# The attention output of a streaming encoder step kept with channels on partitions: gate rows are scaled and turned instead of values

## The reference, cut to what matters

```
oa = _swept_attention(qa, ka, va, _causal, F)          # branch a: softmax over all earlier keys
ob = _banded_sink_attention(qb, kb, vb, sinks)         # branch b: a window of 128 keys back
oc = _swept_attention(qc, kc, vc, _chunk_causal)       # branch c
br = [oa * silu(ga), ob * silu(gb), oc * silu(gc)]     # (tokens, 512) each
up = einsum('bsnw,nwd->bsnd', br, w_br)                # three (512 x 1024) products
mixed = (sigmoid(gates) * up).sum(axis=2)
y = mixed @ w_o ;  x = LayerNorm(alpha * x + y)
```

## Time and profile before

| | |
|---|---|
| median of 3 runs | 3697.83 us (3694.39 to 3703.88) |
| profiled execution, its own time | 3709.84 us |
| its span | 3708.2 us |
| PE (TensorE matmul) busy | 3331.5 us, 90% |
| DVE (VectorE) / ACT (ScalarE) busy | 1433.3 us, 39% / 882.9 us, 24% |
| prompt attention, matmuls first to last | 643.38 to 1420.59 us and 2469.65 to 3242.87 us |
| up projection, SyncE's first load to the last matmul | 1582.54 to 1758.55 us in the first layer |

### The profile page before, as it was taken

How to read it: one execution, slowest core, us unless ns; L and a number is a source line. 1 busy time by engine, 2 the same in 40 slices (tenths; PEclk the granted TensorE clock), 3 DMA queues, 4 the chain that set the end, 5 groups by cost and what they waited for, 6 DMA issues and landing times. The chain is left out here.

```text
span 3708.2 us, 52576 instructions
## 1 busy us (share of the span) xinstructions
PE 3331.5 (90%) x20738; PEld 2665.9 (72%) x20738; DVE 1433.3 (39%) x3527; ACT 882.9 (24%) x1976; POOL 172.6 (5%) x118
## 2 busy tenths in 40 slices
PE   0999987999999996989969999789999999978988
PEld 0788874787777774668758888657777877745877
DVE  5114233444444442354631143334444444424546
ACT  1221211333222332220212212123332233312010
POOL 0000000100110100000000000010011110000000
PEclk9999998999999997989979999889999999978999
DMA  5322215322333317653442222352223332096533
GB/s 196 105 94 88 84 55 175 97 68 56 85 93 86 84 40 183 206 224 125 151 153 85 94 94 67 102 158 71 64 74 85 90 90 66 30 250 224 196 134 108
DMA packets 405676, 419.75 MB, mean 113 GB/s; under 512 B 155072, under 2 KB 314688, under 8 KB 403072
## 3 DMA queue, kind: packets, MB, share of 16 engines
q1 hardware_dynamic: 371600, 376.88, 32.9%
q10 hardware_dynamic: 33840, 39.66, 3.3%
HBM read 291.17 MB, written 127.64 MB: 113 GB/s over the span
## 5 line engine op out<-in xcount | busy, mean ns | idle before, releaser
L1053 PE MATMUL att_gacc<-att_gwh,keep_xh 128*128 128x256 f32 x1728 | 507.5, 294 | 8.3 <-POOL att_gwl L973 8.3
L351 PE MATMUL proj_acc<-proj_wh,keep_xh 128*128 128x512 f32 (+1 forms) x1296 | 502.3, 388 | 12.4 <-DVE proj_wl L326 12.4
L353 PE MATMUL proj_acc<-proj_wh,keep_xl 128*128 128x512 f32 (+1 forms) x1296 | 500.9, 387 | 0.0
L352 PE MATMUL proj_acc<-proj_wl,keep_xh 128*128 128x512 f32 (+1 forms) x1296 | 500.9, 386 | 0.0
L1055 PE MATMUL att_gacc<-att_gwh,keep_xl 128*128 128x256 f32 x1728 | 488.9, 283 | 0.0
L1054 PE MATMUL att_gacc<-att_gwl,keep_xh 128*128 128x256 f32 x1728 | 488.3, 283 | 0.0
L1079 ACT ACTIVATE att_p<-att_ss,att_stat 128x257 f32<-128x257 f32 (+9 forms) x384 | 249.2, 649 | 684.1 <-DVE att_stat L1129 678.2
L1007 PE MATMUL att_ss<-att_kt,att_qt 64*128 64x256 f32 (+9 forms) x1024 | 377.6, 470 | 1.2 <-DVE att_kt L1064 1.2
L1053 PEld LDWEIGHTS att_gacc<-att_gwh,keep_xh 128*128 128x128 f32 x1728 | 329.1, 190 | 24.3 <-issue 10.6
L1054 PEld LDWEIGHTS att_gacc<-att_gwl,keep_xh 128*128 128x128 f32 x1728 | 328.9, 190 | 0.0
L1055 PEld LDWEIGHTS att_gacc<-att_gwh,keep_xl 128*128 128x128 f32 x1728 | 328.2, 190 | 0.0
(11 more groups left out here) (271 smaller groups left out, 4341.4 us busy)
## 6 DMA issues: line engine op xcount, KB each, us to landing
scratch_gates<-att_gout SPq DMA_DIRECT2D x216, 128.0 KB, 1.7
up_gates<-scratch_gates SPq DMA_DIRECT2D x18, 1536.0 KB, 7.6
proj_raw<-in_w_in SPq DMA_DIRECT2D x48, 512.0 KB, 3.7
att_graw<-in_w_in SPq DMA_DIRECT2D x48, 512.0 KB, 3.7
str_ka<-in_cache_a_kT SPq DMA_DIRECT2D x16, 1024.0 KB, 8.6
str_va<-in_cache_a_v SPq DMA_DIRECT2D x16, 1024.0 KB, 5.3
scratch_sg<-proj_out SPq DMA_DIRECT2D x54, 256.0 KB, 2.0
up_br<-scratch_br SPq DMA_DIRECT2D x54, 256.0 KB, 8.0
```

The costliest lines, as they stand in the source:

```text
L351: nc.tensor.matmul(bank, hi, wh[:, u, kt, 0:w], start=kt == 0, stop=False)
L352: nc.tensor.matmul(bank, hi, wl[:, u, kt, 0:w], start=False, stop=False)
L353: mm = nc.tensor.matmul(bank, lo, wh[:, u, kt, 0:w], start=False, stop=kt == KT - 1)
L1053: nc.tensor.matmul(gacc[:, 0:GW], hi, gwh[:, n % 2, k, :], start=k == 0, stop=False)
```

## The change

In attention, `back` is gone. Instead, at the end of each odd turn VectorE takes both reciprocals at once and multiplies the gate rows of the pair with them (`sgr`, tokens on partitions). A new entry `gate(n, a)` transposes `sgr` on TensorE into `tr` and ScalarE copies it to `sgt`. A new entry `mix(n, a)` is one VectorE product of `oo`, straight from PSUM, with `sgt`, into `o`, which now holds channels by tokens. `gate` stands right behind the turn of the next even sub, ahead of the score; `mix` stands behind the score, where `back` was. The store goes to a new scratch tensor `brt` (1536 channels by 1024 tokens). In the up projection the eight prompt tiles are loaded from `brt` with channels on partitions by one DMA each, and ScalarE and VectorE split them straight from SBUF; only the ninth tile is still transposed.

```
@@ attention_order
         for m in range(SUBS):
+            before = None if m % 2 or m + n == 0 else (n, m // 2 - 1) if m else (n - 1, PT - 1)
             order.append(("turn", n, m))
+            if before:
+                order.append(("gate", *before))
             (score as before)
-            if m % 2 == 0 and m:
-                order.append(("back", n, m // 2 - 1))
-            elif m == 0 and n:
-                order.append(("back", n - 1, PT - 1))
+            if before:
+                order.append(("mix", *before))
@@ TensorE
-            def back(n, a):
-                g = groups["back", n, a][0]
-                pe.wait_ge(ot_ready, PT * n + a + 1)
+            def gate(n, a):
+                g = groups["gate", n, a][0]
+                pe.wait_ge(sgr_ready, PT * n + a + 1)
                 bank_free(pe, g)
-                nc.tensor.transpose(tr[:, g % 2, 0:P], ot[:, a % 2, :], C["ident"][:]).then_inc(tr_made, 1)
+                nc.tensor.transpose(tr[:, g % 2, 0:P], sgr[:, a % 2, :], C["ident"][:]).then_inc(tr_made, 1)
@@ ScalarE
+            def gate(n, a):
+                g = groups["gate", n, a][0]
+                act.wait_ge(tr_made, g + 1)
+                if PT * n + a >= 2:
+                    act.wait_ge(o_ready, PT * n + a - 1)
+                nc.scalar.activation(sgt[:, a % 2, :], tr[:, g % 2, 0:P], ACT.Copy).then_inc(tr_taken[g % 2], 1)
@@ VectorE, turn
-                nc.vector.reciprocal(stat[:, m % 4, 2:3], stat[:, m % 4, 1:2]).then_inc(inv_ready, 1)
+                if m % 2:
+                    ...
+                    ch.link(nc.vector.reciprocal(stat[:, both, 2:3], stat[:, both, 1:2]))
+                    nc.vector.tensor_tensor(heads_of(sgr[:, a % 2, :], 2), heads_of(sg[:, n % 2, a, :], 2),
+                                            stat[:, both, 2:3].to_broadcast([P, 2, HD]), ALU.mult).then_inc(sgr_ready, 1)
@@ VectorE, value and back replaced by mix
-                nc.vector.tensor_copy(ot[:, a % 2, :], oo[:, 0:P]).then_inc(ot_ready, 1)
...
-                    nc.vector.scalar_tensor_tensor(out=o[:, a, half], in0=tr[:, g % 2, half],
-                                                   scalar=stat[:, (2 * a + u) % 4, 2:3], in1=sg[:, n % 2, a, half],
-                                                   op0=ALU.mult, op1=ALU.mult).then_inc(sem, 1)
+                nc.vector.tensor_tensor(o[:, rows(a)], oo[:, 0:P], sgt[:, a % 2, :], ALU.mult).then_inc(o_ready, 1)
@@ store, and the load of the up projection
-                    sp.dma_start(dst[:, ts, rows(pair)], o[:, ts, :]).then_inc(o_stored[half], 16)
+                    sp.dma_start(S["brt"][rows(n), tokens], o[:, tokens]).then_inc(o_stored[half], 16)
...
+                if t < PT:
+                    sp.dma_start(brt[:, t % 2], S["brt"].rearrange("(k p) t -> p k t", p=P)[:, :, rows(t)])\
+                        .then_inc(brt_loaded[t % 2], 16)
+                    return
@@ up projection, TensorE
-            turn(0, range(3))
...
-                        if n == 2 and t + 1 < NT:
-                            turn(t + 1, AHEAD[half])
+                        if n == 2 and t + 1 == PT:
+                            turn(AHEAD[half])
```

More of the change, by code:

```diff
@@ L810, in attention_order @@
         assert not ahead
-    order.append(("back", len(UNITS) - 1, PT - 1))
+    order += [("gate", len(UNITS) - 1, PT - 1), ("mix", len(UNITS) - 1, PT - 1)]
     return order
@@ L903, in load_vs @@
                     sp.wait_ge(pv_made, PT * (n - 1))
-                    copied(sp, groups["back", n - 2, PT - 1][0])
+                    sp.wait_ge(sgr_ready, PT * (n - 1))
                 if kind == "b":
@@ L1058, in _ @@
             for what, *of in order:
-                {"prep": prep, "score": score, "turn": turn, "value": value, "back": back, "fill": fill}[what](*of)
+                if what != "mix":
+                    {"prep": prep, "score": score, "turn": turn, "value": value, "gate": gate, "fill": fill}[what](*of)
         def take_prep(eng, copy, n, x, u, half):
@@ L1168, in _ @@
                     turn(*of)
-                elif what == "value":
-                    value(*of)
-                elif what == "back":
-                    back(*of)
+                elif what == "mix":
+                    mix(*of)
     ph.end()
@@ L1768, in _ @@
             for t in range(1, NT):
-                load_rows(t)
+                load_channels(t)
                 load_gates(t)
```

92 lines of the change are left out of this document (46 added, 46 removed).

## The result

| | before | after |
|---|---|---|
| median | 3700.54 us (4 runs, 3694.39 to 3703.88) | 3726.44 us (4 runs, 3721.16 to 3728.44) |
| ratio to the kernel before, 95% interval | | 1.0068 (1.0055 to 1.0081) |
| span of the profiled execution | 3708.2 us | 3726.8 us |
| attention, first to last matmul, layers 1 and 2 | 777.2, 773.2 us | 796.8, 801.1 us |
| last matmul of the stream stage to the last of the up projection | 180.06, 180.58 us | 169.06, 169.39 us |

The change is 0.68% slower, and the time lies above the range that was predicted (3688 to 3720). The direction of each part was as forecast: attention lost, the up projection gained. The loss was larger, 47.4 us instead of 34.1; the gain was nearly as forecast, 22.2 us instead of 23.5 (first layer 1758.55 - 1578.49 against 1757.84 - 1588.78, second 3575.78 - 3395.20 against 3594.32 - 3424.93).

What follows compares the result with a forecast made beforehand. TensorE was taken to bound attention and the up projection's steady tiles. Attention +34.1 and up projection -23.5 give +10.6, less 1 for small waits +9.5: forecast 3707.3 us, range 3688 to 3720.

Steps and rivals of the forecast that it cites:

- the price of the bank wait: Attention, branches a and c: gate ahead of score waits for ScalarE's copy at m = 8, 10, 12; +24.0 us, last units +1.0.
- Branch b, same step: Attention, branch b: gate waits at m = 10, +4.2 us; VectorE's `sgr` product delays m = 8, +2.3 us.
- The small terms: Attention: gate dearer than `back` by 0.05 at 96 subs, +4.8 us; gains of 1.6 at m = 15 and 0.6 at stage end.
- The end of the stage: Attention, from the values to the store: 0.3 us less, up to 0.9 with overlap; -0.6 us for both layers.
- Rival 1: Attention: VectorE's queue becomes late too, in branch b at m = 7, 9, 11; priced at 9 us, 3716 us; chance 0.2.
- Rivals 2 and 3: Delays absorbed except at m = 8, 3691 us, chance 0.14; gate does not wait, having another bank, 3677 us, chance 0.06.
- Up projection: Seven tiles per layer lose transposes, 1.41 us each, -19.7 us; earlier start 1.9 per layer, -3.8; together -23.5 us.
- The sources in SBUF: Up projection start: ScalarE's copies from SBUF cost 52 cycles more than from PSUM, 0.13 us for three; hidden elsewhere.
- Two products and a copy become one product: Attention: what VectorE saves by the change, worth only what TensorE waits for it; no size given.
- the term taken off for delays that meet small waits: In the sum of attention and up projection: 1 us off, from +10.6 to +9.5.
- The case given the chance 0.42: Whole kernel measured slower, over 3708.9 us, by more than the 0.3% that can be told from no change.

Runs made afterwards that it cites:

- the first two experiments: Changed kernel with the gate's transpose behind the score: everywhere, 3708.19 us; only for m of 8 and more in branches a and c, 3705.69 us.
- the experiment with early weights: Changed kernel with gate's transpose behind the score, its copy behind the next exponentials, second half of gate weights loaded mid-unit: 3712.43 us.

## Why the prediction was wrong

- **The failed step: the price of the bank wait. Mechanism right, size too small.** The prediction put TensorE's restart at "the end of that copy, plus 0.06 until TensorE starts". It was 0.15 to the transpose and another 0.13 to the score, 0.22 more than forecast; 0.04 of it comes back because no transpose follows the score any more (0.98 us between the score's old and new place at m = 8, by these numbers, against 0.94 measured). So the forecast of 0.75, 0.22 and 0.53 us at m = 8, 10, 12 became 0.93, 0.40 and 0.73, each 0.18 to 0.20 more. With the last units of a layer, which lose 0.7 to 0.8 more than the others where 0.5 was forecast, that is 34.3 us instead of 25.0. The longer distance could have been read in the earlier trace rows.
- **Branch b, same step.** 0.45 at m = 8 and 0.74 at m = 10 instead of 0.28 and 0.53. With the 0.45 at m = 12 of each layer's last unit, which the prediction did not have, 10.5 us instead of 6.5.
- **The small terms.** The separate 0.05 for each of 96 subs (4.8) showed at three subs a unit, 2.4 us. No delay showed at m = 14, as forecast. The gains were 3.8 us instead of 1.6: 0.11 at m = 15 where 0.1 was forecast, and 0.08 at m = 1 and in branch b, which were not. The end of the stage went as forecast: from the values to the store it takes 0.3 us less.
- **The unit starts and the clock, not in any step.** The starts of the units (m = 2 and 3) make 3.9 us of the 47.4: 6.3 less in branches a and c, 10.2 more in b, where the held products, the gate weights and the fills at 1.2 GHz lie. TensorE's wait for the weights (3 to 5 us a layer before and after) and a half-speed fill behind it were in the trace of the kernel before; they move with the DMA's landing from run to run, and 13 us of attention hung on them there.
- **How it adds up.** Attention lost 13.3 us more than forecast: 9.3 at m = 8, 10 and 12, 4.0 in branch b, 3.9 at the unit starts, less 2.4 and 2.2 for the small terms; 0.7 is spread over other places.
- **Rival 1, VectorE's queue, in part.** It did delay, but by no queue: two products of 2.47 and 2.45 us, held by GpSimd, cost TensorE 1.7 us each. At m = 7, 9 and 11 of branch b, where the rival had its delays, nothing was lost, and the kernel with two places for the gate keeps the product and stands as before the change there. The prediction counted the product at 0.28 and never asked what else runs on SBUF at that time.
- **Rivals 2 and 3, not borne out.** All three delays of a unit reach the turns behind them, so they are not absorbed, and the gate does wait for its bank.
- **Up projection, right.** Forecast -23.5, measured -22.2. The transposes gave 1.41 us a tile as forecast, and the start 1.7 and 2.2 us where 1.9 was forecast: the load took 0.9 and 0.4 us longer, for which 0.5 was taken, and ScalarE's freed work gave 2.6 instead of 2.4. Not foreseen was the wait at the second tile, 1.27 and 1.44 us, where VectorE's remainders stand behind its mixes.
- **The sources in SBUF.** The prediction had three roundings of ScalarE cost 0.13 us more from SBUF than from PSUM, and had no rows for it. The kernel after has both: the rounding of 128x512 takes 617 ns (median) from SBUF and 598 from PSUM, and back to back they start 529 and 494 ns apart, so 0.06 to 0.10 us for the three. VectorE's remainder of the same shape takes 684 and 683 ns.
- **A misreading without weight.** "Two products and a copy become one product": the new kernel has two products a query tile as well (`sgr` and the mix). What VectorE saves is the copy and one reciprocal, 20.8 us of work in the first layer.
- **The sum.** The profiled execution was forecast at 3719.3 and took 3728.44. The medians differ by 25.9 us, and the forecast difference was 9.5. Of the 16.4 between them 13.3 is attention, 1.3 the up projection, and 1.0 the term taken off for delays that meet small waits, which shows at none of the steps; the remaining 0.8 is less than the runs differ among themselves. The case given the chance 0.42, slower by over 0.3%, came true, with a loss of more than twice the forecast.

## What to carry to other kernels

When a step moves within a list that several engines walk, it moves in each engine's queue. Ask for each engine apart which place is free, and give them different places: here the transpose belongs behind the score and the copy ahead of the exponentials, and that split turned a loss of 0.7% into a gain of 0.6%. Price a new wait of TensorE from its release to the second instruction behind it. And ask of each VectorE instruction with both inputs in SBUF which GpSimd instruction may run beside it; splitting that one, or moving it to where nobody waits, bounds the damage. The version that beats both kernels (3657.0 us, 1.3% under the kernel before) is the change with the two places and the gate weights half a unit earlier (its earlier load of the second tile changed nothing); the weights alone gave the old kernel 0.3%.

## What the runs showed of the hardware that I had not expected

- A VectorE product of 128x128 with both inputs in SBUF took 2.42 to 2.47 us where a GpSimd subtraction of 128x1024 started 0.02 to 0.07 us ahead of it, 0.29 otherwise. Wherever in GpSimd's instruction a held product began, up to 2.1 us into it, it ended 0.14 to 0.15 us behind that instruction, in every run. With pieces of 128x256 the longest was 0.82. GpSimd's cast holds it as well: one product that started 0.28 us into a cast took 0.90 and ended 0.15 behind it.
- Which unit starts collide shifts with half a microsecond: 14 held products in the changed kernel, 19 and 20 in the first two experiments, with four to five times the time. Two orders should not be compared on this alone from one trace.
- A transpose that is the first of its entry and waits for its PSUM bank starts 0.14 to 0.15 us behind the end of the copy that frees it (20 waits before, 72 after); a further group of the same turn 0.05 to 0.06 (40 in each).
- Idle gaps of about 1 us between short matmuls at a unit's start in branch b (the experiment with early weights) were followed by 7 to 10 us at 1.2 GHz; a gap of 2.4 us for gate weights by 3.4 us of it. At that clock a fill of 24 matmuls starts its last 4.3 us behind its first instead of 2.8.
- The first load of the up projection, one DMA with pieces of 512 bytes, landed 4.9 to 5.2 us behind its issue in every kernel with the change. Three loads of the same 786 KB in larger pieces took 4.1 and 4.6 us in the kernel before and 4.3 and 5.3 in the same kernel with early weights. The difference of 0.46 us between the means is about the 0.5 that the prediction took, not the 0 that follows from the rule of the Trainium skill cited there (DMA: Bandwidth & Descriptors, Specifications: 512 bytes suffice for line rate); but one DMA and three differ in more than their pieces, so its cause is open.
